# Expert loop of TensorE closed behind a second gate/up tile, token transposes grouped by shape, high and low products of a tile in pairs

## What is computed

```python
def expert_choice_ffn(h, w_router, w_gate_e, w_up_e, w_down_e):
    aff = jax.nn.softmax((h @ w_router).astype(jnp.float32), axis=-1)
    gates, idx = lax.top_k(aff.T, cap)
    xe = h[idx]
    def one_expert(args):
        xc, wg, wu, wd = args
        a = xc @ wg
        b = xc @ wu
        return (jax.nn.silu(a) * b) @ wd
    ye = lax.map(one_expert, (xe, w_gate_e, w_up_e, w_down_e))
    ye = ye * gates[..., None].astype(ye.dtype)
    return jnp.zeros_like(h).at[idx.reshape(-1)].add(ye.reshape(-1, D))
```

## Time and profile before

| | |
|---|---|
| median of 3 runs | 2915.82 us (2914.61 to 2916.9) |
| span of the profiled execution, first to last instruction | 2913.2 us |
| mean granted TensorE clock | 0.956 |
| busy share of the span: PE, PEld, DVE, ACT, POOL | 91%, 75%, 58%, 42%, 31% |
| HBM read and written | 462.28 MB and 24.87 MB |

### The profile page before, as it was taken

One profiled execution on the slowest core, in us unless ns is written; L12 is line 12 of the kernel. 1 busy time (PEld: TensorE's weight loads), 2 busy tenths in 40 slices (PEclk: granted clock), 3 DMA queues, 4 the chain that ended last, 5 costly groups with the idle time before them and its releaser, 6 DMA issues.

```text
span 2913.2 us, 46659 instructions
## 1 busy us (share of the span) xinstructions
PE 2660.3 (91%) x17898; PEld 2197.9 (75%) x17898; DVE 1681.9 (58%) x2075; ACT 1229.0 (42%) x1685; POOL 903.3 (31%) x352
## 2 busy tenths in 40 slices
PE   7999999999999999479989899998999999899997
PEld 4456677676777768368888888888888888888887
DVE  3011422432110143677987887797788779778876
ACT  2011333332000021145665565566566556656554
POOL 0004111110111000234344444434444443443443
PEclk9999999999999999789999999999999999999999
DMA  7211010010110143347787787778778777877872
GB/s 234 40 27 40 17 34 21 6 36 4 40 43 22 29 178 125 144 149 255 266 269 250 258 265 250 258 269 266 249 257 278 250 249 269 268 253 252 287 249 68
DMA packets 340356, 489.78 MB, mean 168 GB/s; under 512 B 22090, under 2 KB 194777, under 8 KB 340192
## 3 DMA queue, kind: packets, MB, share of 16 engines
q1 hardware_dynamic: 332864, 461.60, 46.9%
q0 software_dynamic: 7328, 25.58, 4.1%
HBM read 462.28 MB, written 24.87 MB: 167 GB/s over the span
## 4 chain that ended last, share of the span: by engine, by line
PE 62%; issue 23%; DVE 11%; ACT 2%; DMA 1%; SPq 0%; DVEq 0%; POOL 0%; ACTq 0%; POOLq 0%
PE ps L1267 28%; PE ps L1524 15%; PE ps L1527 7%; PE ps L1447 4%; PE ps L1372 3%; DVE gu L1200 2%; DVE act_f L1207 2%; PE ps L1385 2%; DVE w_lo L434 1%; DVE act_b L1213 1%; DVE act_hl L1215 1%; ACT w_hi L855 1%; PE ps L1514 1%; PE ps L1332 1%; DMA spos_s_sb<-in_spos_s 1%
## 5 line engine op out<-in xcount | busy, mean ns | idle before, releaser
L434 POOL TENSOR_TENSOR w_lo<-raw,w_hi 128x2048 bf16<-128x2048 f32 x132 | 635.5, 4816 | 800.7 <-ACT w_hi L855 800.7
L1524 PE MATMUL ps<-x_hl,w_hi 128*128 128x320 f32 x4112 | 755.9, 327 | 128.4 <-issue 78.3
L855 ACT ACTIVATE w_hi<-raw 128x2048 fp32r<-128x2048 f32 x388 | 739.2, 1906 | 3.0 <-issue 3.0
L1524 PEld LDWEIGHTS ps<-x_hl,w_hi 128*128 128x128 f32 x4112 | 630.2, 195 | 146.0 <-issue 82.6
L434 DVE TENSOR_TENSOR w_lo<-raw,w_hi 128x2048 bf16<-128x2048 f32 x256 | 624.8, 2441 | 96.0 <-ACT w_hi L855 96.0
L1527 PE MATMUL ps<-x_b,w_lo 128*128 128x160 bf16 x4112 | 382.6, 237 | 0.0
L1524 PE MATMUL ps<-act_hl,w_hi 128*128 128x320 f32 x2048 | 349.0, 322 | 0.0
L1527 PEld LDWEIGHTS ps<-x_b,w_lo 128*128 128x128 bf16 x4112 | 279.0, 100 | 54.0 <-issue 3.2
L1524 PEld LDWEIGHTS ps<-act_hl,w_hi 128*128 128x128 f32 x2048 | 311.9, 194 | 2.0
L1207 DVE TENSOR_TENSOR act_f<-silu,gu 128x160 f32<-128x160 f32 x256 | 213.7, 835 | 19.4 <-ACT silu L880 19.4
L873 ACT ACTIVATE lows<-ps 128x320 f32<-128x320 f32 x256 | 111.0, 434 | 254.9 <-PE ps L1527 253.7
(11 more groups left out here) (179 smaller groups left out, 2997.0 us busy)
## 6 DMA issues: line engine op xcount, KB each, us to landing
raw<-in_w_g SPq DMA_DIRECT2D x64, 2048.0 KB, 9.0
raw<-in_w_u SPq DMA_DIRECT2D x64, 2048.0 KB, 11.4
raw<-in_w_d SPq DMA_DIRECT2D x64, 2048.0 KB, 9.1
m_raw<-in_w_in SPq DMA_DIRECT2D x16, 512.0 KB, 4.7
h_raw<-in_w_in SPq DMA_DIRECT2D x12, 512.0 KB, 4.0
x_in<-in_x SPq DMA_DIRECT2D x10, 512.0 KB, 4.2
x_res<-in_x SPq DMA_DIRECT2D x10, 512.0 KB, 4.1
y_out<-x SPq DMA_DIRECT2D x10, 512.0 KB, 2.9
```

The source lines that it names most:

```text
L434: engine.tensor_tensor(unit(w_lo, v), raw_half(v), unit(w_hi, v).bitcast(F32), ALU.subtract)\
L855: act.activation(unit(w_hi, w), raw_half(w), ACT.Copy).then_inc(hi_ready, 1)
L1524: pe.matmul(out, unit(w_hi, v)[:, k, cols], hl[:, k, :, :].rearrange("p a n -> p (a n)"), start=k == 0, stop=False)
```

## The change

It is made in TensorE's stream alone. Three edits:

1. `expert_transposes` runs over the 8 prompt chunks first and over the 8 sample chunks behind them.
2. `split_product` is cut in two, `high_product` and `low_product`. A tile of gate and up now makes the 8 + 8 high products of both banks and then the 8 + 8 low ones. The wait for the second unit stands before the second 8 high products.
3. Two tiles (0 and 1) stand ahead of the loop. The body begins at tile 2 and ends with tiles 0 and 1 of the next expert. `back(7)` stands between the high and the low products of that tile 0.

```diff
                 for b, k0, kn in X_BANKS:
                     for k in range(k0, k0 + kn):
-                        col = CAP * (k - k0)
-                        pe.transpose(bank(b, P, first=col), xg_p[:, P * k:P * k + P], ident[:, :])
-                        op = pe.transpose(bank(b, CAP_S, first=col + P), xg_s[:, P * k:P * k + P],
+                        pe.transpose(bank(b, P, first=CAP * (k - k0)), xg_p[:, P * k:P * k + P], ident[:, :])
+                for b, k0, kn in X_BANKS:
+                    for k in range(k0, k0 + kn):
+                        op = pe.transpose(bank(b, CAP_S, first=CAP * (k - k0) + P), xg_s[:, P * k:P * k + P],
                                           ident[0:CAP_S, 0:CAP_S])
                 op.then_inc(x_tr, 1)
 
-            def split_product(out, n, v, cols, hl, b, part=None):
-                part = part or range(n)
+            def high_product(out, v, cols, hl, part):
                 for k in part:
                     pe.matmul(out, unit(w_hi, v)[:, k, cols], hl[:, k, :, :].rearrange("p a n -> p (a n)"),
                               start=k == 0, stop=False)
+            def low_product(out, n, v, cols, b, part):
                 for k in part:
                     op = pe.matmul(out[:, CAP:2 * CAP], unit(w_lo, v)[:, k, cols], b[:, k, :],
                                    start=False, stop=k == n - 1)
                 return op
 
-            def tile_of_gate_and_up(e, j):
-                b = 2 * (j % 2)
+            def tile_of_gate_and_up(e, j, between=None):
+                b, v, cols = 2 * (j % 2), j // 2 * 2, slice(P * (j % 2), P * (j % 2) + P)
                 for n in range(2):
-                    v = j // 2 * 2 + n
                     if j % 2 == 0:
-                        wait_split(pe, e, v)
-                    op = split_product(bank(b + n, 2 * CAP), KT, v, slice(P * (j % 2), P * (j % 2) + P), x_hl, x_b)
+                        wait_split(pe, e, v + n)
+                    high_product(bank(b + n, 2 * CAP), v + n, cols, x_hl, range(KT))
+                if between is not None:
+                    between()
+                for n in range(2):
+                    op = low_product(bank(b + n, 2 * CAP), KT, v + n, cols, x_b, range(KT))
                 op.then_inc(gu_ready, 1)
...
             tile_of_gate_and_up(0, 0)
+            tile_of_gate_and_up(0, 1)
             with pe.Fori(0, EXPERTS) as e:
-                for j in range(1, FT):
-                    if j >= 2:
-                        pe.wait_ge(gu_added, e * FT + (j - 1))
+                for j in range(2, FT):
+                    pe.wait_ge(gu_added, e * FT + (j - 1))
                     tile_of_gate_and_up(e, j)
...
                 pe.wait_ge(x_ready, e + 2)
                 pe.wait_ge(y_ready, e * 4 + 3)
-                tile_of_gate_and_up(e + 1, 0)
-                back(KT - 1)
+                tile_of_gate_and_up(e + 1, 0, between=lambda: back(KT - 1))
+                tile_of_gate_and_up(e + 1, 1)
```

More of the change, by code:

```diff
@@ L1573, in _ @@
                             pe.wait_ge(act_ready, e * 8 + k1 // 2)
-                            op = split_product(out, FT, 16, slice(0, P), act_hl, act_b, range(k0, k1))
-                    else:
-                        op = split_product(out, FT, 16 + d, slice(0, P), act_hl, act_b)
+                            high_product(out, 16, slice(0, P), act_hl, range(k0, k1))
+                            op = low_product(out, FT, 16, slice(0, P), act_b, range(k0, k1))
+                    else:
+                        high_product(out, 16 + d, slice(0, P), act_hl, range(FT))
+                        op = low_product(out, FT, 16 + d, slice(0, P), act_b, range(FT))
                     op.then_inc(down_ready, 1)
```

## The result

The changed kernel takes **3007.1 us** (median of 4 runs, 3005.59 to 3017.76), against 2915.45 for the kernel before on the same chip: ratio 1.0322, 95% interval 1.0308 to 1.0335. It is 92 us slower. The forecast was 2910.3, its range 2897 to 2922.

The account below looks back on a forecast made before the run. PE was taken as the bound, idle at the branch back (73.7 us) and waiting for gu (42.7 us). Last restart -4.6 and the part behind it -0.9 made -5.5 us, from 2915.8 to 2910.3 us, range 2897 to 2922.

Parts of the forecast that it names:

- the seam: Between two experts, at the loop's branch back: moving tile 1 ahead of the stall brings no gain in itself.
- the cover of the branch: Work still queued on PE while the branch is held: now only low products, +0.37 us idle an expert, bounds -0.5 and +0.9.
- Sum at the old head: Whole kernel: all terms together make it 5.5 us faster, 2910.3 us.
- Beat of 102.40 us: PE's clock rises every 102.40 us, one expert; the low clock grows to 5.0 us and eats each expert's gain.
- Stall of the branch: PE's idle time at the branch back: 5.55 us start to start, against 4.91 + 0.27 before; "issue" stalls near 5.3 us.
- Pairs: Gate and up, highs of both banks then lows: saves 0.054 us in each of 16 tiles, of which 0.45 an expert counts.
- the ring: Gate and up: PE, ACT, POOL and DVE wait on each other; one of three tiles counts, the other two's savings become wait.
- Transposes: Token transposes grouped by shape: 1.96 us less on PE, turned into wait for yT(0); gain 0, or -0.4 on average.
- The clock falls at `back(0)`: Rival, chance 0.15: PE's 2.5 us wait in down drops the clock, tile 2 loses 1.5 us; about 2934, or 2922.
- One rise later: Rival, chance 0.14: first restart misses the clock rise at 1371.2, later ones follow 3.4 us later; -2, about 2914 us.
- Start and end: Once each: first transposes -1.0 us at the start; output rows ready earlier by `back(7)`, -1.2 us at the end.

Follow-up runs that it names:

- e15: Kernel before with only the rotation (tile 1 moved ahead of the loop, `back(7)` between the two), nothing added: 2989.46 us, ratio 1.0253.
- e2: Kernel before with 64 idle semaphore increments ahead of its expert loop, so its head stands where the change has it: 3012.04 us, ratio 1.0328.
- e9: Changed kernel with 192 idle increments at a place where PE waits anyway, head back where it was before the change: 2912.14 us, ratio 0.9986.
- e12: Changed kernel with PE's loop over the experts written out 16 times, so no branch back: 2883.25 us, ratio 0.9884.
- e1: Changed kernel with 16 idle increments right before the first expert, head 10 instructions into the next block: 2881.42 us, ratio 0.9881.
- e5: Kernel before with 80 idle increments right before the first expert, head 10 instructions into a block: 2881.08 us, ratio 0.9876.
- e8: Changed kernel with 16 idle increments right before the first expert and the transposes in turn as before the change: 2876.26 us, ratio 0.9869.
- e10: Kernel before with the high and low products in pairs and 80 idle increments at the covered place: 2890.27 us, ratio 0.9907.
- e13: Kernel before with 80 idle increments at the covered place, head 10 instructions into a block: 2875.25 us, ratio 0.9863.
- e14: Kernel before with only the rotation and 16 idle increments at the covered place, head 10 instructions into a block: 2874.56 us, ratio 0.9859.
- e7: Changed kernel with 150 idle increments right before the first expert, head 144 instructions into a block: 2895.42 us, ratio 0.9931.
- e6: Changed kernel with 192 idle increments right before the first expert, head 186 instructions into a block as in the kernel before: 2935.89 us, ratio 1.0072.
- e11: Kernel before with 50 idle increments at the covered place, head 236 instructions into a block, 20 left: 2984.58 us, ratio 1.0234.
- e17: Kernel before with the rotation and the transposes grouped by shape, no pairs, nothing added: 2994.57 us, ratio 1.0279.
- e4: Kernel before with the high and low products of a tile in pairs alone, head unmoved: 2915.93 us, ratio 0.9994.
- e3: Kernel before with the transposes grouped by shape alone, head unmoved: 2914.12 us, ratio 0.9992.

## Why the prediction was wrong

**The step that failed is the seam:** "Tile 1 goes ahead of the stall and tile 2 pays the low clock for it: no gain in itself", with +0.37 us for the cover of the branch and bounds "-0.5 and +0.9, by the spread of the branch". That step asked what lies ahead of the branch and who needs tile 1. It took the 6.46 us of the branch as a price that stays, whatever stands behind it. What stands behind it is what the rotation changes: the loop's head moved by 64 instructions, and of 70 that had covered the fetch of the next block 6 were left. The term was +0.37 us an expert, and with it the period was to stay at 102.4; measured the period is 6.6 longer (109.03 - 102.43), 99 us in 15 seams, and 4.7 of the 6.6 are the second stall itself. By the rotation alone (e15) the loss is 74 us, by the place of the head alone (e2) 95. The bounds came from the spread of one kind of stall and could hold no second one. No rival had it; the range missed for that reason, since with the old head the same three edits land in it (e9).

Two signs were there. The groups of the sequencer show one loop whose branch takes 208 ns and one with 6458; the prediction noted that the long one must be fetched again and did not ask in what units. And the page of the profile of the kernel before gives its instruction queue 153 packets:

```profile
q8 instruction: 153, 2.51, 0.4%
```

How the units follow from the runs: e12's 113 packets against the 18 of the kept loop are 95 for 15 more bodies of 1632 instructions (800 products and transposes, two each, and 32 others by my count), 258 to a packet. The traces have 41 or 42 others in a body; with them it is 259. With 256 to a block, a body of 1632 lies within seven blocks (1792) if its head is at most 160 instructions into one (150 by the traces' count). The runs have 10 (e1, e5, e8, e10, e13, e14) and 144 (e7): branch in 0.21 us. Heads at 186 (before, e6, e9), 236 (e11) and 250 (the change, e2, e15 to e17) reach into an eighth, and the branch is held 6.3 to 6.5 us at the median. No run has a head between 144 and 186, so the runs bracket the edge and don't hit it. The 153 packets less 18 are 135, nine for each of 15 branches. That is the eight blocks of the body and one more: the whole body is fetched again each time. The Trainium skill, "Runtime: NRT & Kernel Launch", section Instruction fetch mechanics, gives PE a store of 128 KiB, 2048 instructions, refilled in blocks of 256, prefetched in sequence alone. The runs agree with the block, and with a store of eight if one of them is always being filled; that last is argued, not shown. By the same page's window of two blocks a body of seven would have to be fetched too; e13 shows that it is not.

The other steps, by e9 (the same three edits with the head in its old place) and the changed kernel:

- **Sum at the old head.** -5.5 us predicted, 4.1 faster measured (1.5 to 6.7). That they agree so well is partly luck: the terms below for the start and for the low clock were each off by 0.5 us or more, and executions of e9 differ by 10 us (2909.99 to 2920.31).
- **Beat of 102.40 us.** e9 has 102.40. The gain of an expert goes into a longer low clock, as forecast: 5.0 us behind the restart were predicted, and in e9's second seam the stretch below has 0.54 on the mean, (1 - 0.54)/0.5 x 6.0 = 5.5 us.

```profile
1475.40:1481.40 6.00, 5.93 (x31) 5.74 (x32) 4.71 (x2) 0.00 (x0) 5.11 (x3) 0.54 0.62 121
```

- **Stall of the branch.** 5.55 us start to start, or 5.3 of idle time predicted; 5.25 in the changed kernel, 76.7/15 = 5.1 in e9.
- **Pairs.** Four waits for gu an expert, each a little longer: 0.88 us on the mean (52.9/60) against 0.76 (42.7/56 in the earlier trace rows). The saving on PE is there: a tile of the changed kernel takes 3.51 us (starts at 1605.54 and 1609.05), as forecast. It goes into the ring, as put. Alone it is worth nothing that shows (e4). That it costs 13 us where the seam is free (e10) the prediction did not see; it needed a wait for the split that no row of before had.
- **Transposes.** 1.46 us from start to start predicted, 1.58 measured (1652.11 to 1653.69); the two spacings that the prediction names make only 8 x 0.109 + 8 x 0.064 = 1.38, and it does not say what the other 0.08 are. Wait for yT(0) 2.5 predicted, 2.43 measured; gain 0. Right, and e3 shows it alone.
- **The clock falls at `back(0)`** (rival, chance 0.15). It happens in the changed kernel, 4.00 us for 16 highs against 2.59, about the 1.5 us that it was priced at. But it isn't the main cause of the loss: the grouping with the rotation adds 0.0026 to the ratio, about 8 us (e15, e17). The question that the prediction put, "whether 2.5 us is enough", has no single answer: behind the same wait the clock falls in 1 expert of 16 in e3 and in 15 in the changed kernel.
- **One rise later** (rival, chance 0.14). Its 3.4 us stand in no row of the prediction. The runs show such a step: 105.8 - 102.4, and 109.2 - 105.8.
- **Start and end.** From the first transposes to the first tile 7.55 us (1256.02 to 1263.57, in the changed kernel) against 9.83 in the earlier trace rows: -2.3, forecast -1.0. From the start of the last tile 0 to the end of the span the change saves 1.3 us (17.8 against 19.1), forecast -1.2.

## What to carry to other kernels

In this kernel a hardware loop of 1632 instructions on PE cost no stall, 4.9 us of stall, or 8 to 10 us an expert, by the place of its head alone. Before a change moves work across such a loop's head or alters its length, count the instructions to the next block boundary and the blocks that the body touches; a branch record of several us and the packets of the instruction queue tell that the body is fetched again. A few idle instructions at a covered place ahead of the loop can be worth more than the edit (here 80 of them, 1.4%), and unless the heads stand alike, two versions of the order can't be compared.

## What the hardware showed that I had not expected

- The same body of 1632 instructions branches back in 0.21 us with its head 10 or 144 instructions into a block and in 6.3 to 6.5 us with it 186, 236 or 250 into one; by the count above that is seven blocks or eight.
- Behind a refetched head the next block comes 5.2 to 5.8 us after the restart at the seams shown. 6 instructions left in the first block cover 0.9 us of it (stalls of 4.89 in e2, 4.30 in the changed kernel), 20 cover 2.6 (3.15 in e11), 70 cover it all.
- Straight-line code of 16 bodies (e12) ran without a stall of fetching in the expert part, at 1632 instructions in some 100 us.
- An increment of a semaphore takes PE 0.15 us (192 in 28.9), where a covered place makes it free.
- With the seam stalled, an expert took 102.4, 105.8 or 109.2 us from one fall of the granted clock to the next, and no length in between was seen.
